# A decoder layer on one NeuronCore: the hidden activations turned by VectorE and through DRAM, in place of TensorE's transposes

## The reference, cut to what matters

```
x = x + 0.5 * swiglu(rmsnorm(x), w1_gate, w1_up, w1_down)      # d_ff = 5632
z = rmsnorm(x) @ w_in
x = x + concat(mla(z), rwkv7(z)) @ w_out
x = x + 0.5 * swiglu(rmsnorm(x), w2_gate, w2_up, w2_down)      # d_ff = 5632
x = x + sigmoid(rmsnorm(x) @ w_ple_gate) * (p @ w_ple_proj)

swiglu(h, g, u, d) = (silu(h @ g) * (h @ u)) @ d
```

## Time and profile before

| | |
|---|---|
| median of three runs | 2014.79 us |
| the profiled execution: its own time | 2014.49 us |
| the profiled execution: span from first to last instruction | 2012.7 us |
| mean granted TensorE clock of the execution | 0.997 |
| TensorE matmuls busy | 1979.8 us, 98% of the span |
| VectorE busy | 1506.6 us, 75% |
| ScalarE busy | 1071.8 us, 53% |
| DMA queue of SyncE and ScalarE (q1) | 361.48 MB, 52.9% of 16 engines' span |
| DMA queue of GpSimd (q0) | 53.09 MB, 13.9% |

### The profile page before, as it was taken

How to read it: one execution, slowest core, us unless ns; L and a number is a source line. 1 busy time by engine, 2 the same in 40 slices (tenths; PEclk the granted TensorE clock), 3 DMA queues, 4 the chain that set the end, 5 groups by cost and what they waited for, 6 DMA issues and landing times.

```text
span 2012.7 us, 28994 instructions
## 1 busy us (share of the span) xinstructions
PE 1979.8 (98%) x11176; PEld 1638.6 (81%) x11176; DVE 1506.6 (75%) x1324; ACT 1071.8 (53%) x1043; POOL 233.3 (12%) x190
## 2 busy tenths in 40 slices
PE   8999999999999999999898999999999999999999
PEld 6788888888888889888787888888888888888887
DVE  5987787778878755766788546988878777787664
ACT  4655555555555556855344346555555555555553
POOL 0000000000000000344432000000000000000000
PEclk9999999999999999999998999999999999999999
DMA  7587668776787756667312555678766877677854
GB/s 249 195 242 232 215 220 249 230 232 211 235 239 233 216 174 219 198 191 222 120 42 71 173 188 168 197 241 241 237 213 209 250 234 234 211 234 231 239 178 147
DMA packets 214636, 415.69 MB, mean 207 GB/s; under 512 B 11207, under 2 KB 21059, under 8 KB 214557
## 3 DMA queue, kind: packets, MB, share of 16 engines
q1 hardware_dynamic: 189116, 361.48, 52.9%
q0 software_dynamic: 25440, 53.09, 13.9%
HBM read 363.94 MB, written 5.52 MB: 184 GB/s over the span
## 4 chain that ended last, share of the span: by engine, by line
PE 90%; DVE 7%; issue 2%; ACT 1%; DMA 0%; SPq 0%; DVEq 0%; ACTq 0%
PE PS L466 14%; PE PS L468 14%; PE PS L467 14%; PE PS L541 8%; PE PS L543 8%; PE PS L542 8%; PE PS L559 6%; PE PS L558 6%; PE PS L560 6%; PE PS L1638 2%; DVE wlo L426 2%; PE PS L521 1%; PE PS L487 1%; ACT t_hi L448 1%; DVE t_lo L453 0%
## 5 line engine op out<-in xcount | busy, mean ns | idle before, releaser
L426 DVE TENSOR_TENSOR wlo<-raw,whi 128x2048 fp32r<-128x2048 f32 (+2 forms) x338 | 732.5, 2167 | 337.3 <-PE PS L468 271.3
L417 ACT ACTIVATE whi<-raw 128x2048 fp32r<-128x2048 f32 (+2 forms) x338 | 606.0, 1794 | 217.2 <-PE PS L468 137.2
L541 PE MATMUL PS<-whi,xT_hi 128*128 128x512 f32 x768 | 303.8, 396 | 4.9 <-issue 3.2
L543 PE MATMUL PS<-whi,xT_lo 128*128 128x512 f32 x768 | 300.8, 392 | 0.0
L542 PE MATMUL PS<-wlo,xT_hi 128*128 128x512 f32 x768 | 299.4, 390 | 0.0
L466 PE MATMUL PS<-whi,hT_hi 128*128 128x512 f32 x680 | 267.6, 394 | 0.6 <-DVE wlo L426 0.4
L448 ACT ACTIVATE t_hi<-T 128x2048 fp32r<-128x2048 f32 x80 | 153.7, 1922 | 214.2 <-DVE T L443 214.2
L468 PE MATMUL PS<-whi,hT_lo 128*128 128x512 f32 x680 | 265.2, 390 | 0.0
L467 PE MATMUL PS<-wlo,hT_hi 128*128 128x512 f32 x680 | 264.8, 389 | 0.0
L1391 POOL DMA_DIRECT2D x_resid<-xs x80 | 96.1, 1202 | 1196.5 <-ACT xs L694 1159.9
L453 DVE TENSOR_TENSOR t_lo<-T,t_hi 128x2048 fp32r<-128x2048 f32 x80 | 183.4, 2292 | 31.6 <-ACT t_hi L448 31.6
(11 more groups left out here) (383 smaller groups left out, 2786.3 us busy)
## 6 DMA issues: line engine op xcount, KB each, us to landing
raw<-in_w_up SPq DMA_DIRECT2D x176, 512.0 KB, 4.0
raw<-in_w_gate SPq DMA_DIRECT2D x176, 512.0 KB, 4.9
raw<-in_w_down SPq DMA_DIRECT2D x88, 1024.0 KB, 5.1
x_resid<-xs POOLq DMA_DIRECT2D x80, 512.0 KB, 6.9
raw<-in_w_in SPq DMA_DIRECT2D x28, 1024.0 KB, 5.5
raw<-in_w_out SPq DMA_DIRECT2D x16, 1024.0 KB, 5.1
raw<-in_w_ple_gate SPq DMA_DIRECT2D x16, 1024.0 KB, 5.2
raw<-in_w_q_b SPq DMA_DIRECT2D x3, 1024.0 KB, 5.7
```

Of the source, the lines that this page charges most:

```text
L417: nc.scalar.activation(whi[:, n % WHI, a:wd], raw[:, n % RAW, a:wd], ACT.Copy).then_inc(hi_ready, 1)
L426: nc.vector.tensor_tensor(wlo[:, n % WLO, a:wd], raw[:, n % RAW, a:wd], f32(whi[:, n % WHI, a:wd]), ALU.subtract).then_inc(lo_ready, 1)
L541: nc.tensor.matmul(PS[:, bank, :], a, whi[:, n % WHI, c], start=first, stop=False)
L543: return nc.tensor.matmul(PS[:, bank, :], b, whi[:, n % WHI, c], start=False, stop=last)
```

## The change

VectorE transposes h in 32 by 32 blocks (its transpose can't cross a group of 32 partitions). SyncE stores the result in a DRAM scratch of 512 KB and loads it back in four DMAs, one for each group of 32 partitions, which put the blocks where they belong. ScalarE and VectorE then make `hT_hi` and `hT_lo` from SBUF and not from PSUM.

- `h_turn` moves from TensorE to VectorE: two transposes of 128x512 right behind `hidden` (and behind `first_hidden` for tile 0).
- SyncE issues `store_h` behind the load of the next pass's block 0, and `load_hT` behind that of its block 1. For tile 0 they stand behind the loads of blocks 4 and 5 of pass 0, for the last product behind its first two loads.
- `hT_part_hi` moves from the head of a pass to behind ScalarE's split of block 3 (pass 0: of block 6), and `hT_part_lo` to behind VectorE's `forms_lo` of block 3 (pass 0: behind its split of block 6). In pass 9 they stay where they were for the last product.
- TensorE waits for `hT_ready` only at the first down block. Its waits for the PSUM banks that the transposes wrote go.
- `hT`, the loaded tile, shares its place with `G`. `h_quads`, 4 KB a partition, is new.

```
+        hT = sb("hT", [P, 4, FKT * TT, 32], at=G0)
+        h_quads = sb("h_quads", [P, 4, FKT, TT, 32])
+        h_dram = nc.dram_tensor("h_scratch", [P, TT * COLS], F32, kind="Internal").ap()
-        def h_turn(pe, f, i, it=0, b=2):
-            pe.wait_ge(h_ready, NFF * f + i + 1 + it)
-            for j in range(FKT):
-                for t in range(TT):
-                    ins = nc.tensor.transpose(PS[:, b + j // 2, (j % 2) * SEQ + t * P:(j % 2) * SEQ + (t + 1) * P],
-                                              h[:, t, j * P:(j + 1) * P], ident)
-            ins.then_inc(h_turned, 1)
...
                     ins.then_inc(block_used, 1)
-                    if (i, v) == (0, 0):
-                        h_turn(pe, f, 0)
                     continue
                 first, last = v == 1, v == 7
+                if (i, v) == (0, 1):
+                    pe.wait_ge(h_ready, NFF * f + 1)
...
-                if v == 1:
-                    pe.wait_ge(hT_ready, NFF * f + i + 1 + it)
...
             for j in range(4):
-                if turn_next and j == 2:
-                    pe.wait_ge(x_evac, evacs(f, i, 0))
-                    h_turn(pe, f, i + 1, b=0)
+                if j == 0:
+                    pe.wait_ge(hT_ready, NFF * f + i + 1 + it)
...
             if i:
-                pe.wait_ge(x_evac, evacs(f, i - 1, 1) + 4 * it)
-                h_turn(pe, f, i, it)
                 pe.wait_ge(x_evac, evacs(f, i - 1, 2) + 4 * it)
...
+        def by_quads(a):
+            return a.rearrange("p (n a c) -> p n a c", n=FKT * TT, a=4)
+        def hT_part_hi(act, f, i, it=0, dst=None):
+            act.wait_ge(hT_moved, 64 * (NFF * f + i + 1) + 64 * it)
+            if i:
+                act.wait_ge(block_used, FFN_BASE[f] + PAIRS + 12 * i - (4 if dst else 0) + 12 * it)
+            nc.scalar.activation(by_quads((dst or hT_hi)[:, :, :].rearrange("p k s -> p (k s)")),
+                                 hT[:, :, :, :].rearrange("p a n c -> p n a c"), ACT.Copy).then_inc(hT_hi_ready, 1)
...
+        def h_turn(dve, f, i, it=0):
+            dve.wait_ge(h_ready, NFF * f + i + 1 + it)
+            for t in range(TT):
+                ins = nc.vector.transpose(h_quads[:, :, :, t, :].rearrange("p q k r -> p k q r"),
+                                          h[:, t, :].rearrange("p (k q r) -> p k q r", k=FKT, q=4))
+            ins.then_inc(h_turned, 1)
...
                 if s in (0, 2, 4, 6):
                     forms_lo(dve, n + s + 1, it)
+                if s == (2 if i else 5):
+                    hT_part_lo(dve, f, i, it)
...
                 if s == 8:
                     hidden(dve, f, i, it)
+                    h_turn(dve, f, i + 1, it)
...
+            def store_h(f, i, it=0):
+                sp.wait_ge(h_turned, NFF * f + i + 1 + it)
+                sp.dma_start(h_dram, h_quads[:, :, :, :, :].rearrange("p q k t r -> p (q k t r)")).then_inc(h_stored, 16)
+            def load_hT(f, i, it=0):
+                sp.wait_ge(h_stored, 16 * (NFF * f + i + 1) + 16 * it)
+                for q in range(4):
+                    sp.dma_start(hT[32 * q:32 * q + 32, :, :, :].rearrange("p a n c -> p a (n c)"),
+                                 h_dram[:, q * 256:(q + 1) * 256].rearrange("(a r) x -> r a x", a=4)).then_inc(hT_moved, 16)
...
                         load_unit(sp, n + v, g, u, c, it)
+                        if i is not None and v == (0 if i else 4):
+                            store_h(f, i, it)
+                        if i is not None and v == (1 if i else 5):
+                            load_hT(f, i, it)
...
                         load_block(sp, n + j, ...)
+                        if i is not None and j == 0:
+                            store_h(f, i)
+                        if i is not None and j == 1:
+                            load_hT(f, i)
```

More of the change, by code:

```diff
@@ L208, in phase @@
             base[0] = R0
+        G0 = base[0]
         G = sb("G", [P, 4, COLS])
+        hT = sb("hT", [P, 4, FKT * TT, 32], at=G0)
         TLO0 = base[0]
@@ L593, in pe_units, with down @@
                 seven_product(m, P5, True, first, last).then_inc(block_used, 1)
-        def down(pe, f, i, it=0, last=False, turn_next=False):
+        def down(pe, f, i, it=0, last=False):
             n = FFN_BASE[f] + PAIRS + 12 * i + (0 if last else PAIRS)
@@ L661, in pe_ffn @@
                 pe_pass(pe, f, 1, it)
-            pe_pass(pe, f, NFF - 2, turn_next=True)
+            pe_pass(pe, f, NFF - 2)
             down(pe, f, NFF - 1, last=True)
@@ L717, in act_pass @@
                     down_out(act, f, i - 1, 3, it)
-                    hT_part_hi(act, f, i, it)
                 if s in (0, 2, 4, 6):
@@ L727, in act_pass @@
                 split_hi(act, n + s + 2, it)
-                if s == 0 and not i:
-                    hT_part_hi(act, f, 0)
+                if s == (1 if i else 4):
+                    hT_part_hi(act, f, i, it)
                 if s == 3 and not i:
@@ L732, in act_pass @@
                 if turn_next and s == 10:
-                    hT_part_hi(act, f, i + 1, dst=last_hT_hi, b=0)
+                    hT_part_hi(act, f, i + 1, dst=last_hT_hi)
         def act_ffn(act, f, B):
@@ L793, in hidden, with hT_part_lo @@
             ins.then_inc(h_ready, 1)
-        def hT_part_lo(dve, f, i, it=0, dst=None, hi=None, b=2):
+        def h_turn(dve, f, i, it=0):
[4 more added lines that the diff above has]
+            ins.then_inc(h_turned, 1)
+        def hT_part_lo(dve, f, i, it=0, dst=None, hi=None):
             dve.wait_ge(hT_hi_ready, NFF * f + i + 1 + it)
-            nc.vector.tensor_tensor((dst or hT_lo)[:, :, :].rearrange("p (b j) s -> p b (j s)", b=2), PS[:, b:b + 2, :],
-                                    f32((hi or hT_hi)[:, :, :]).rearrange("p (b j) s -> p b (j s)", b=2),
-                                    ALU.subtract).then_inc(hT_ready, 1)
+            flat = "p k s -> p (k s)"
+            nc.vector.tensor_tensor(by_quads((dst or hT_lo)[:, :, :].rearrange(flat)),
+                                    hT[:, :, :, :].rearrange("p a n c -> p n a c"),
+                                    by_quads(f32((hi or hT_hi)[:, :, :]).rearrange(flat)), ALU.subtract).then_inc(hT_ready, 1)
         def update_x(dve, n, j, factor, it=0):
@@ L851, in dve_pass @@
                     split_lo(dve, n + s + 1, it)
-                if s == 0 and i:
-                    hT_part_lo(dve, f, i, it)
                 if s in (0, 2, 4, 6):
                     forms_lo(dve, n + s + 1, it)
-                if s == 0 and not i:
-                    hT_part_lo(dve, f, 0)
+                if s == (2 if i else 5):
+                    hT_part_lo(dve, f, i, it)
                 if s == 3 and not i:
@@ L867, in dve_pass @@
                     hidden(dve, f, i, it)
+                    h_turn(dve, f, i + 1, it)
                 if turn_next and s == 10:
-                    hT_part_lo(dve, f, i + 1, dst=last_hT_lo, hi=last_hT_hi, b=0)
+                    hT_part_lo(dve, f, i + 1, dst=last_hT_lo, hi=last_hT_hi)
         def dve_ffn(dve, f, B):
@@ L890, in dve_ffn @@
             first_hidden(dve, f, B)
+            h_turn(dve, f, 0)
             dve_pass(dve, f, 0)
```

18 lines of the change are left out of this document (9 added, 9 removed).

## The result

The changed kernel takes 2037.95 us (median of five runs, 2032.88 to 2040.7) against 2014.79 us. The ratio, taken over all ten executions and not from the medians, is 1.0108, with a 95% interval of 1.0091 to 1.0124. The forecast was 2005.3 us with a range of 1997 to 2017: wrong in sign and outside the range.

The account below looks back on a forecast made before the run. TensorE was taken to bound the kernel. Turns removed (-15.7 and -1.7), pass 0 (+2.1) and last-product stalls (+5.8) gave -9.5 us, from 2014.8 to 2005.3 us; range 1997 to 2017, leaving out the late weight loads.

Parts of the forecast that it names:

- What bounds the kernel: Whole kernel: TensorE sets the time, with a matmul in flight for 1979.8 of 2012.7 us.
- removed from TensorE: Turns of h leaving TensorE at 0.87 us each: 15.7 us for 18 pass heads, 1.7 for two last products.
- VectorE, passes 1 to 9: Heads of passes 1 to 9: VectorE's turn takes 1.40 us, block 10's split keeps 0.7 us to spare, nothing lost.
- Pass 0: First pass of each layer: work added to VectorE ahead of block 9 is paid in full, 2.1 us together.
- My sign to look for: Pass 0: TensorE's idle time before block 9 would be 1.4 us, not 0.2.
- SyncE and the DMA queue: Weight loads behind the store and loads of h in the loop passes: a loss of nothing, 1.1 us spare at worst.
- My worst case: Loop pass: block 14's second load lands at 451.4 at the latest, against 452.5 when needed.
- The slow rival: Weight loads late in every pass: 1.2 us in each of 18 passes, +22, 2027 us; chance 0.17.
- The last product: End of each layer: the turned h arrives late and TensorE stalls 2.9 us, 5.8 together; bounds 0 and 5.5 each.
- The sum: Whole kernel: -15.7 - 1.7 + 2.1 + 5.8 = -9.5 us, giving 2005.3 us.

Follow-up runs that it names:

- no_trip: The changed kernel without the store and loads of the turned h, both halves split from VectorE's own tile (wrong rows): 1994.85 us, ratio 0.9905.
- late_again: late_trip repeated unchanged in five rounds: 1993.96 us, ratio 0.9889 to the kernel before.
- late_pass0: late_trip with the turn of pass 0 given back to VectorE and the DRAM trip: 1997.51 us, ratio 0.9913 to the kernel before.
- tiny_both: The changed kernel with its waits, but store and loads cut to 128 bytes a partition, halves split from VectorE's tile (wrong rows): 2003.96 us, ratio 0.9945.
- act_queue: The changed kernel with ScalarE instead of SyncE issuing the store and four loads, same bytes and pieces: 2034.70 us, ratio 1.0107.
- late_trip: The changed kernel with store and loads behind blocks 5 and 6's loads in passes 1 to 9; TensorE turns pass 0 and last product: 1993.80 us.
- mid_trip: late_trip with store and loads two places earlier, behind the loads of blocks 3 and 4: 1994.26 us, ratio 0.9897 to the kernel before.
- last_only: The kernel before with only each layer's last product turned by VectorE and through DRAM: 2026.87 us, ratio 1.0057.

## Why the prediction was wrong

**What bounds the kernel**, **removed from TensorE**: right. Each hidden turn gives 0.93 us, 16.7 for 18 and 1.8 for the last two. The forecast was 15.7 and 1.7.

**VectorE, passes 1 to 9**: right for the turn. The transposes took 691 ns (forecast 710), with block 10's split done in time, and TensorE never waited there. Its next split has 1.14 us of idle time left of the 2.41 in the earlier trace rows, here in pass 0, whose transposes turn tile 1:

```profile
112.41 1.30 DVE L794 STREAM_TRANSPOSE h_quads<-h 128x512 f32<-128x512 f32 x2
113.64 2.25 DVE L431 TENSOR_TENSOR wlo<-raw,whi 128x2048 fp32r<-128x2048 f32 x1
117.03 2.29 DVE L431 TENSOR_TENSOR wlo<-raw,whi 128x2048 fp32r<-128x2048 f32 x1 [1.14 <-PE PS L473]
```

The new place of `hT_lo` was right only where block 15 came in time (no_trip). Behind a late block 15 VectorE has no idle time to give it, and it costs, as shown above.

**Pass 0**: right in kind, 2.1 forecast, 3.5 measured between the medians of late_again and late_pass0 and 1.7 between their profiles. My sign to look for was wrong: the idle time before block 9 is 0.24 us, because TensorE had already lost its time in block 1 (1.15), block 7 (0.17) and before block 8 (0.49), in the timeline of TensorE:

```profile
70.40 0.50 PE L555 MATMUL PS<-t_hi,more_hi 128*128 128x512 f32 x1 [1.15 <-DVE t_lo L458]
101.73 0.50 PE L555 MATMUL PS<-t_hi,more_hi 128*128 128x512 f32 x1 [0.17 <-DVE t_lo L458]
105.27 0.47 PE L471 MATMUL PS<-whi,hT_hi 128*128 128x512 f32 x1 [0.49 <-DVE G L765]
111.19 0.47 PE L471 MATMUL PS<-whi,hT_hi 128*128 128x512 f32 x1 [0.24 <-DVE wlo L431]
```

**SyncE and the DMA queue**: here the prediction failed. It said "I take a loss of nothing, with 1.1 us to spare at worst". The stalls in the passes are 8 x 1.30 + 8 x 1.09 and 1.6 + 1.7 in pass 9, together 22.4 us. Three things were wrong in it: which blocks it followed, what a megabyte costs, and where between its bounds it put the loss.

- It followed block 14 and stopped. Block 14 came at 5.0 to 6.4 us behind the start of the pass. My worst case was 451.4 - 446.4 = 5.0, and my limit 6.1, so it was at its limit, and it lost 4.6 us in all. Block 15 stands behind it in the same queue, is odd, and so needs VectorE's sums and two splits before use. It came 11.0 us behind the start (median), 5.9 later than in no_trip, and has to land by 10.7. Behind it `hT_lo` delays the split of block 16 by 1.22 us. These two blocks lost 17.6 us, and the prediction has neither. Since block 16's stalls are 0.5 us each, they would be gone for the most part with `hT_lo` elsewhere. That is an estimate from these rows; no run has a late block 15 without it.
- It priced the megabyte at 5.3 us. Blocks 14 and 15 moved by 5.9 against no_trip, with most of block 15's by the store alone.
- A loss of "nothing" between 0 and a worst case that left 1.1 us was no middle. The slow rival was late weight loads, priced at 1.2 us a pass and +22 in all. It had a chance of 0.17, and the range left it out. That the stalls sum up to 22.4 is luck: the price was worked out for block 14, where only 4.6 us of them arise. Its trigger was wrong, too: it named SyncE's standing still and the 1 KB pieces. SyncE's waits cost the passes nothing when they carry no bytes (tiny_both); act_queue, which moves them to ScalarE, gives back 0.2 to 0.3 us a pass, and the pieces are a small part.

**The last product**: right in kind, mis-sized. The forecast was 2.9 us each within 0 to 5.5. Measured were 28.61 - 22.05 = 6.6 and 28.30 - 22.05 = 6.3, and then 2.0 and 2.5 us in the stage behind it, of which the prediction has nothing. The chain of it, forecast and measured from the turn's end: store landed after 5.4 and 6.7; four issues 1.9 and 3.5; the last piece landed after 4.8 and 5.7. Each link was taken too short. The lone store's 3.1 us, and with it the rule of 2.0 us fixed and the rest by bytes that the Trainium skill has ("DMA: Bandwidth & Descriptors", Anatomy of one DMA), doesn't give the time of a DMA behind weights: the same 512 KB took 5.7 to 6.6 us here, and 16 KB took 4.5.

**The sum** from measured parts, all of the profiled execution: -16.7 - 1.8 + 2.5 (pass 0) + 22.4 + 12.9 + 4.4 = +23.7 us. With the 5.0 less between the layers that is 18.7, against 18.4 in the span. The medians differ by 23.2; the median execution is 5 us longer than the profiled one, and no trace shows where. That 23.7 lies close to 23.2 is chance.

The Trainium skill's rule for kernel authors ("VectorE: DVE Perf Modes", Rules for kernel authors), TensorE for a 128x128 transpose where PSUM will do, came out on the right side for this change as it stands. Yet late_trip breaks it for 18 of 22 turns and gains 1% (0.9903; in its repeat 0.9889, 0.9873 to 0.9906), since TensorE is the engine that never rests and VectorE still has 10 us a pass.

Still open: why the store delays block 15 by more than its share of bytes (writes to DRAM beside the accumulating DMAs is a guess, not tried by itself), what the changed kernel would take with `hT_lo` moved alone, and why its executions spread over 8 us.

## What to carry to other kernels

Before putting a DMA into a queue, list every later load with its landing and its last useful time, and add the delay to each down to the end of the full stretch; the tightest is often not the next one, but one with extra steps before its use. If a trip is needed late, put it behind the tight loads: here the trip three places later in the order (mid_trip), with `hT_lo` behind block 6's split and the turns of pass 0 and of the last products left on TensorE, was worth 44 us. Ask the same of what was put on the engines behind such a load. A round trip through DRAM in a busy queue was 16 us from the turn to the landed data, so it fits a loop pass of 63 us and not a tail of four blocks.

## What the runs showed of the hardware

- A stall of TensorE costs twice. In the change's first layer, in an idle time of 6.45 us, its granted clock fell to 0.50 (711 to 712) and rose again between 718 and 719, after 4 us of matmuls at half the clock; the next stage was 2.0 us longer, and 2.5 in the second layer. In tiny_both, with ends of 24.82 and 24.25 against 22.05, it was 0.51 from 699.00 to 702.00 in the first layer, and stayed at 1.00 in the second. The Trainium skill ("TensorE: Matmul & The Clock Gate", What's actually happening) has two states, 1.2 GHz when idle and 2.4 GHz when busy; the trace agrees with 0.50 and 1.00.
- Part of the time between the two layers seems to go with the program: 474.8 and 476.5 us in two profiles of the kernel before, 469.9 to 473.3 in all others, though nothing was changed there. In the two, TensorE has a gap of 1.72 and 2.00 us put down to "issue" in the RWKV part, at 1101.00 and 1104.16, that late_trip and its repeat lack. But last_only has one of 1.43 us at another line and 471.5 in all, so the gap isn't the whole of it. What makes such gaps come and go wasn't tried. Some 3 to 6 us of late_trip's gain of 20 are of this kind by these profiles.
- The four issues of a turn's loads took SyncE 1.9 to 3.8 us in the change, with a median of 3.0, and 1.76 in late_trip's emptier stretch (median; at most 2.5), for the same descriptors.
